# Expert bodies of a mixture-of-experts layer: down products and scatter moved one body later, two weight loads moved earlier

## The chip, the cores and the metric

The kernel runs on one core of a Trainium2 chip. The metric is the device time of one execution in microseconds. Before the change three runs gave 671.87, 671.91 and 672.01 us, median 671.91 us.

## The reference

One decoder layer over 512 tokens of width 1024, in float32. An attention branch and a gated linear attention branch are merged and added to the residual `h`; that part is not touched here. What follows is a mixture of experts: 4 groups of 8 experts, the best group, in it the two best experts.

```python
g_idx = argmax(xn @ router_group);  top_v, top_i = top_k(logits of that group, 2)
combine = softmax(top_v) * softmax(group logits)[g_idx]        # one weight per token and chosen expert
for g, e in 32 experts:                                        # FF = 256
    hg = silu(xn @ w_gate[g, e]) * (xn @ w_up[g, e])
    y += (hg * combine[:, g, e]) @ w_down[g, e]
return h + y
```

Each expert has 3 MiB of weights: gate, up and down, 1 MiB each. All 32 are read, 96 MiB.

## The kernel before

**Work.** Every expert takes up to 64 tokens (slots) in a round; the trace shows one round. Two experts stand side by side in one set of 128 slots and are called a pair; a body (`BODIES` = 8) works on two pairs, `s` = 0 and 1. In PE's order a body is:

1. gate and up products of pair 0, in two parts of 16 matmuls, into PSUM bank 0 (`expert_gate_up`, L990);
2. gate and up products of pair 1 into bank 1, and between their two parts the small products that give the row numbers and routing weights of the body after next (`slot_values`, L953), the transposes of the first pair's hidden rows (L998) and those of a one-hot matrix of slots (L960);
3. down products, 16 for each pair (L1004), with the second pair's hidden transposes among them;
4. transposes of the next body's gathered token rows (`row_transposes`, L984);
5. the scatter: 32 matmuls with the transposed one-hot matrix that put the slots' results back to their tokens (L1114), in two parts, `y_hi` and `y_lo`, whose sum is the float32 value.

Around PE: ScalarE takes SiLU of the gates (`hs`, L1452), copies the transposed hidden rows and one-hots out of PSUM (L1445, L1435), and rounds the down result to `y_hi` (L1465). VectorE multiplies `hs`, up product and routing weight (`hg`, L1880), forms `y_lo` (L1903), weights the transposed rows of the next body into `xgT` (L1862), adds the scattered rows to `h` (L1916), and builds one-hots (L1820) and row numbers (L1531, L1533). GpSimd gathers each pair's token rows from HBM by those row numbers (L2031). The eight PSUM banks are shared out by the constants `GU_BANK` to `LAST_BANKS`.

**Weights.** There is one buffer per pair of a body (`w_pair`), for gate and up together and for down. SyncE requests weights in a written order (`load`, L1146): when the gate products of pair `s` are done it loads the next body's gates of that pair (4 MiB), when the down products are done the next downs (2 MiB a pair). All go on one queue. The first body's weights lie in memory that the layer's earlier part still uses, so they are loaded in pieces as it comes free; down weights of its second pair come last, behind the picking of the first body's rows (`s_pick`, L943).

**Before the experts** the last token block is routed, the first body's rows are picked by matmuls with a one-hot matrix, and the routing weights of the last two blocks are formed on VectorE (`weigh`, the last line of it L1524), for which the products of the first slot weights (`first_slot_weights`) wait.

Of the kernel before, what the change touches and what calls it, by code (L numbers as in the profile page):

```python
# [53 lines left out]
H_BANK = (2, 3)  # L54
DOWN_BANKS = ((4, 5), (6, 7))
ROWS_BANKS = (0, 1, 2, 3)
W_BANKS = (4, 7)
OH_BANK = (5, 6)
SCATTER_BANKS = (4, 7, 5, 6)
LAST_BANKS = (0, 1, 2, 3, 4, 5, 6, 7)  # L60
# [197 lines left out]
def layer_kernel(nc, x, meta_tokens, norm1_w, w_in, q_norm_w, k_norm_w, attn_sinks, gla_gate_up, gla_gate_bias,  # L258
                 gla_norm_w, w_attn_branch, w_gla_branch, w_out, norm2_w, router_rows, norm2_rows,
                 expert_w_gate, expert_w_up, expert_w_down, table, triangle, rows_hbm, out):  # L260
    with ExitStack() as ctx:
# [138 lines left out]
        pause = more("pause", [P, 9])  # L400
# [6 lines left out]
        onehot = more("onehot", [P, NB, 2 * P], BF16)  # L407
# [190 lines left out]
        flipped = [tiles[k][:, 0:2 * P].bitcast(BF16) for k in OH_BANK]  # L598
# [5 lines left out]
        def _(pe):  # L604
# [343 lines left out]
            def oh(s, b):  # L948
                return onehot[:, b, s * P:(s + 1) * P]

            def slot_matmul(s, j, a, z):
                for b in range(NB):
                    last = nc.tensor.matmul(tiles[W_BANKS[s]][:, a:z], oh(s, b), info[:, b, 2 * j + s, a:z],  # L953
                                            start=(b == 0), stop=(b == NB - 1))
                return last

            def onehot_transposes(into=flipped):
                for s in range(2):
                    for b in range(NB):
                        last = nc.tensor.transpose(into[s][:, b * P:(b + 1) * P], oh(s, b), ident_b[:, :])  # L960
                    last.then_inc(s_ohTm[s], 1)
# [4 lines left out]
            onehot_transposes(first_flipped)  # L966
            pe.wait_ge(s_rounds, 1)
            rounds = pe.value_load(rounds_i[0:1, 0:1], min_val=1, max_val=T // SLOT)
            with pe.Fori(0, rounds) as r:
# [5 lines left out]
                def row_transposes(j):  # L975
                    for s in range(2):
                        pe.wait_ge(s_xg[s], 16 * (r * BODIES + j))
                        for half in range(2):
                            g = 2 * s + half
                            if j == BODIES:  # L980
                                pe.wait_ge(s_add[g], (r + 1) * (2 * BODIES))
# [14 lines left out]
                def hidden_transposes(s):  # L996
                    for f in range(2):
                        last = nc.tensor.transpose(tiles[H_BANK[s]][:, f * P:(f + 1) * P], hg[s][:, f * P:(f + 1) * P], ident)  # L998
                    last.then_inc(s_hTm[s], 1)
# [31 lines left out]
                def first_slot_weights():  # L1031
# [5 lines left out]
                    for s in range(2):  # L1037
                        pe.wait_ge(s_idx[s], r * BODIES + 1)
                        last = slot_matmul(s, 0, 2, 8)
                    last.then_inc(s_pwm, 1)  # L1040

                for i in range(BODIES):
                    n = r * BODIES + i

                    pe.wait_ge(s_xgT[0], n + 1)
                    pe.wait_ge(s_wgu[0], 64 * n + 64)
                    expert_gate_up(i, 0, 0)
                    if i == 0:
                        first_slot_weights()
                    pe.wait_ge(s_xgT[1], n + 1)  # L1050
                    expert_gate_up(i, 0, 1).then_inc(s_gu[0], 1)
                    if i == 0:
                        pe.wait_ge(s_pw, n + 1)
                        slot_values(1)
                        for s in range(2):
                            pe.wait_ge(s_ohT[s], n + 1)
                        onehot_transposes()
                    pe.wait_ge(s_xgT[2], n + 1)
                    pe.wait_ge(s_wgu[1], 64 * n + 64)
                    expert_gate_up(i, 1, 0)  # L1060
                    pe.wait_ge(s_xgT[3], n + 1)
                    for k in range(4):
                        pe.wait_ge(s_add[k], 2 * n + 1)
                    if i == 0:
                        pe.wait_ge(s_pw, n + 2)
                    if i + 2 < BODIES:
                        slot_values(i + 2)
                    elif i + 1 == BODIES:
                        for s in range(2):
                            pe.wait_ge(s_oh[s], n + 2)  # L1070
                            slot_matmul(s, 0, 0, 2).then_inc(s_tkm[s], 1)
                    pe.wait_ge(s_hg[0], n + 1)
                    hidden_transposes(0)
                    if i == 0:
                        for s in range(2):
                            pe.wait_ge(s_ohT[s], r * BODIES + 2)
                    if i + 2 != BODIES:
                        onehot_transposes()
                    expert_gate_up(i, 1, 1).then_inc(s_gu[1], 1)

                    if i + 2 < BODIES:
                        pe.wait_ge(s_pw, n + 3)
                        for s in range(2):
                            pe.wait_ge(s_ohT[s], r * BODIES + i + 3)
                    elif i + 1 == BODIES:
                        for s in range(2):
                            pe.wait_ge(s_idx[s], n + 2)
                            pe.wait_ge(s_ohT[s], n + 2)
                    pe.wait_ge(s_hT[0], n + 1)
                    pe.wait_ge(s_wd[0], 32 * n + 32)  # L1090
                    expert_down(0, 0)
                    pe.wait_ge(s_hg[1], n + 1)
                    hidden_transposes(1)
                    expert_down(0, 1).then_inc(s_down[0], 1)
                    pe.wait_ge(s_hT[1], n + 1)
                    pe.wait_ge(s_wd[1], 32 * n + 32)
                    expert_down(1, 0)
                    expert_down(1, 1).then_inc(s_down[1], 1)

                    if i + 1 == BODIES:  # L1100
                        last_scatter(i, n)
                        row_transposes(i + 1)
                        continue
                    row_transposes(i + 1)
                    for s in range(2):
                        pe.wait_ge(s_ylo[s], n + 1)
                    for u in range(8):
                        b, half = u // 2, u % 2
                        if u >= 4:
                            pe.wait_ge(s_add[u % 4], 2 * n + 2)  # L1110
                        cols_ = slice(half * 512, (half + 1) * 512)
                        for s in range(2):
                            for part in (y_hi, y_lo):
                                last = nc.tensor.matmul(tiles[SCATTER_BANKS[u % 4]][:, :], onehotT[i % 3][s][:, b, :],  # L1114
                                                        part[s][:, cols_], start=(s == 0 and part is y_hi),
                                                        stop=(s == 1 and part is y_lo))
                        last.then_inc(s_sc[u % 4], 1)

        @block.sync
        def _(sp):  # L1120
# [27 lines left out]
            def reload(i, n):  # L1148

                for s in range(2):  # L1150
                    sp.wait_ge(s_gu[s], n)
                    load(2 * i + s, s, True)
                for s in range(2):
                    sp.wait_ge(s_down[s], n)
                    load(2 * i + s, s, False)

# [10 lines left out]
            load(1, 1, True)  # L1167
            store_rows(NB - 1)
# [3 lines left out]
            load(1, 1, False)  # L1172
            with sp.Fori(1, BODIES) as i:
                reload(i, i)
            sp.wait_ge(s_rounds, 1)
            rounds = sp.value_load(rounds_i[0:1, 0:1], min_val=1, max_val=T // SLOT)
            with sp.If(rounds > 1):
                with sp.Fori(1, rounds) as r:
                    with sp.Fori(0, BODIES) as i:
                        reload(i, r * BODIES + i)  # L1180
# [9 lines left out]
        def _(act):  # L1190
# [29 lines left out]
            for step in SCHEDULE:  # L1220
# [186 lines left out]
                elif kind == "rowhi":  # L1407
                    b = step[1]
                    if b == NB - 1:
                        act.wait_ge(s_ohr, b)  # L1410
                        nc.scalar.activation(onehot[:, 0:b, :], onehot_r[:, 0:b, :].bitcast(F32), ACT.Copy).then_inc(s_cast, 1)
# [8 lines left out]
            nc.scalar.activation(onehot[:, NB - 1, :], onehot_r[:, NB - 1, :].bitcast(F32), ACT.Copy).then_inc(s_cast, 1)  # L1420
# [11 lines left out]
            def onehot_out(j, m, out_of=flipped):  # L1432
                for s in range(2):
                    act.wait_ge(s_ohTm[s], m + 1)
# [655 lines left out]
```

## Time and profile before

| | |
|---|---|
| median of the runs | 671.91 us |
| span of the profiled execution | 669.75 us (669.8 on the page) |
| PE busy | 650.2 us, 97% |
| PE in the chain that ended last | 87% of the span |
| VectorE, ScalarE busy | 390.7 us (58%), 215.9 us (32%) |
| expert weights requested | 96 loads of 1 MiB on SyncE's queue |
| rows gathered | 16 indirect DMAs, 3.64 MB |
| granted TensorE clock from 24 us on | 1.00 |

The span runs from the first to the last instruction of one profiled execution. Its share lines cut the span in 40 slices of 16.7 us; the experts fill about slices 25 to 40. "Busy" is the time in which an engine has an instruction at work; for PE the ends are modelled, so starts are the better measure of its pace.

### The profile page before, as it was taken

The numbers are of one execution on the slowest core, as the hardware profiler recorded it, in microseconds if no ns is written. First come the engines' busy times: TensorE is split into PE (matmuls) and PEld (weight loads), VectorE is DVE, ScalarE is ACT, GpSimd is POOL, SyncE is SP. The second block draws the span as 40 slices with busy tenths as digits, with TensorE's granted clock in tenths as the row PEclk, the third lists the DMA queues.
The fourth block names the chain that finished last, engine by engine and source line by source line (L and its number), as shares of the span: only waits on it lengthen the run. The fifth ranks groups of instructions, "written<-read, shape, count | busy, mean of one in ns | idle before, by whom it ended". The sixth has DMA issues, their size and how long they took to land.

```text
span 669.8 us, 10196 instructions
## 1 busy us (share of the span) xinstructions
PE 650.2 (97%) x3969; PEld 466.9 (70%) x3969; DVE 390.7 (58%) x736; ACT 215.9 (32%) x448; POOL 101.4 (15%) x138
## 2 busy tenths in 40 slices
PE   5799999999999999999989999999999999999998
PEld 3579999988888888888779995354544445453535
DVE  4648335678897878785674667453443535251615
ACT  6346232234534444422435565302020201110112
POOL 3300015899300000000000010110110101010010
PEclk9899999999999999999999999999999999999999
DMA  7432223202232121112345057999999999999943
GB/s 242 147 125 65 64 65 97 92 1 64 79 100 74 60 68 52 68 44 90 126 166 243 33 219 284 381 408 412 401 422 397 423 394 420 407 418 404 417 185 126
DMA packets 49794, 138.72 MB, mean 207 GB/s; under 512 B 6202, under 2 KB 28235, under 8 KB 41556
## 3 DMA queue, kind: packets, MB, share of 16 engines
q1 hardware_dynamic: 47298, 134.37, 52.8%
q0 software_dynamic: 2304, 3.64, 1.5%
q8 instruction: 32, 0.52, 0.3%
q14 instruction: 14, 0.11, 0.1%
q10 hardware_dynamic: 146, 0.07, 0.0%
HBM read 138.62 MB, written 4.19 MB: 213 GB/s over the span
## 4 chain that ended last, share of the span: by engine, by line
PE 87%; DVE 6%; ACT 3%; issue 2%; DMA 1%; POOL 0%; ACTq 0%; DVEq 0%
PE bank L990 16%; PE bank L608 12%; PE bank L609 12%; PE bank L610 12%; PE bank L1004 8%; PE bank L1114 8%; PE bank L850 1%; DVE y_lo L1903 1%; PE bank L1015 1%; PE bank L877 1%; PE bank L874 1%; ACT whi L1233 1%; DVE sig_a L1617 1%; DVE sig_a L1613 1%; DMA wraw<-in_w_out 1%
## 5 line engine op out<-in xcount | busy, mean ns | idle before, releaser
L990 PE MATMUL bank<-w_pair,xgT 128*64 128x512 f32 x512 | 113.8, 596 | 0.0
L990 PEld LDWEIGHTS bank<-w_pair,xgT 128*64 128x64 f32 x512 | 35.2, 137 | 66.4 <-issue 65.4
L1547 DVE TENSOR_TENSOR wlo<-wraw,whi 128x2048 fp32r<-128x2048 f32 (+1 forms) x25 | 56.4, 2258 | 20.3 <-ACT whi L1233 20.3
L608 PE MATMUL bank<-whi,xhi 128*128 128x256 f32 x224 | 64.4, 288 | 0.0
L609 PE MATMUL bank<-wlo,xhi 128*128 128x256 f32 x224 | 63.0, 281 | 0.0
L610 PE MATMUL bank<-whi,xlo 128*128 128x256 f32 x224 | 62.9, 281 | 0.0
L608 PE MATMUL bank<-xhi,whi 128*128 128x512 f32 x152 | 61.4, 404 | 0.0
L609 PE MATMUL bank<-xlo,whi 128*128 128x512 f32 x152 | 60.1, 396 | 0.0
L610 PE MATMUL bank<-xhi,wlo 128*128 128x512 f32 x152 | 59.7, 393 | 0.0
L1004 PE MATMUL bank<-w_pair,hT 128*64 128x512 f32 x256 | 58.1, 595 | 0.0
L1880 DVE SCALAR_TENSOR_TENSOR hg<-bank,pair_w,hs 128x256 f32<-128x256 f32 x16 | 7.7, 483 | 80.6 <-ACT hs L1452 80.6
L1233 ACT ACTIVATE whi<-wraw 128x2048 fp32r<-128x2048 f32 (+1 forms) x25 | 46.6, 1870 | 24.9 <-PE bank L617 11.1
L1452 ACT ACTIVATE hs<-bank 128x256 f32<-128x256 f32 x16 | 6.1, 384 | 135.5 <-PE bank L990 135.5
L1916 DVE TENSOR_TENSOR h<-h,bank 128x512 f32<-128x512 f32 x64 | 41.4, 681 | 7.5 <-PE bank L1114 6.0
L1114 PE MATMUL bank<-y_hi,onehotT 128*128 128x512 f32 x112 | 44.2, 394 | 1.5 <-DVE y_lo L1903 1.5
L1114 PE MATMUL bank<-y_lo,onehotT 128*128 128x512 f32 x112 | 43.7, 390 | 0.0
L1903 DVE TENSOR_TENSOR y_lo<-bank,y_hi 128x512 fp32r<-128x512 f32 x32 | 20.6, 685 | 39.2 <-ACT y_hi L1465 39.2
L608 PEld LDWEIGHTS bank<-whi,xhi 128*128 128x128 f32 x224 | 42.1, 188 | 1.8 <-issue 1.4
L610 PEld LDWEIGHTS bank<-whi,xlo 128*128 128x128 f32 x224 | 42.2, 188 | 0.0
L609 PEld LDWEIGHTS bank<-wlo,xhi 128*128 128x128 f32 x224 | 42.1, 188 | 0.0
L1004 PEld LDWEIGHTS bank<-w_pair,hT 128*64 128x64 f32 x256 | 17.7, 137 | 33.3 <-issue 33.3
L1927 POOL TENSOR_TENSOR pause<-pause 128x1 f32<-128x1 f32 x34 | 6.0, 196 | 223.0 <-PE bank L984 184.1
(331 smaller groups left out, 1330.9 us busy)
## 6 DMA issues: line engine op xcount, KB each, us to landing
w_pair<-in_expert_w_gate SPq DMA_DIRECT2D x32, 1024.0 KB
w_pair<-in_expert_w_up SPq DMA_DIRECT2D x32, 1024.0 KB
w_pair<-in_expert_w_down SPq DMA_DIRECT2D x32, 1024.0 KB, 17.4
wraw<-in_w_in SPq DMA_DIRECT2D x17, 1024.0 KB, 5.6
wraw<-in_w_out SPq DMA_DIRECT2D x4, 1024.0 KB, 5.3
h<-in_x SPq DMA_DIRECT2D x4, 512.0 KB, 5.3
wraw<-in_w_gla_branch SPq DMA_DIRECT2D x2, 1024.0 KB, 5.0
wraw<-in_w_attn_branch SPq DMA_DIRECT2D x2, 1024.0 KB, 5.2
```

The lines of the kernel that those rows point to most:

```text
L608: nc.tensor.matmul(ps, lhi(k), rhi(k), start=(k == 0), stop=False)
L609: nc.tensor.matmul(ps, lhi(k), rlo(k), start=False, stop=False)
L610: last = nc.tensor.matmul(ps, llo(k), rhi(k), start=False, stop=(k == kt - 1))
L850: nc.tensor.matmul(ps[:, 0:width], q, k, start=True, stop=True).then_inc(banks.done(("S", b, i, j)), 1)
L990: last = nc.tensor.matmul(tiles[GU_BANK[s]][j * SLOT:(j + 1) * SLOT, :].rearrange("p (f n) -> p f n", f=2), xgT[:, k, s * P + j * SLOT:s * ...
L1004: last = nc.tensor.matmul(tiles[DOWN_BANKS[s][half]][j * SLOT:(j + 1) * SLOT, :], hT[s][:, f, j * SLOT:(j + 1) * SLOT], we[s][j][2][:, f, ...
L1114: last = nc.tensor.matmul(tiles[SCATTER_BANKS[u % 4]][:, :], onehotT[i % 3][s][:, b, :], part[s][:, cols_], start=(s == 0 and part is y_hi ...
L1233: nc.scalar.activation(wh, raw, ACT.Copy).then_inc(s_hi, 1)
L1547: nc.vector.tensor_tensor(wl, raw, wh.bitcast(F32), ALU.subtract).then_inc(s_lo, 1)
L1880: nc.vector.scalar_tensor_tensor(hg[s][:, :], tiles[GU_BANK[s]][:, FF:2 * FF], pair_w[:, 2 * i + s:2 * i + s + 1], hs[s][:, :], ALU.mult, ...
L1903: last = nc.vector.tensor_tensor(y_lo[s][:, cols_], tiles[DOWN_BANKS[s][half]][:, :], y_hi[s][:, cols_].bitcast(F32), ALU.subtract)
L1916: nc.vector.tensor_tensor(h[:, b, cols_], h[:, b, cols_], tiles[bank][:, :], ALU.add).then_inc(s_add[u % 4], 1)
```

## The change

The order of PE, ScalarE, VectorE and SyncE in the experts is written anew. Down products and scatter of body `i` move into body `i + 1`; only body 0 keeps its own down products, and the last body does both its predecessor's and its own. Gate and up products of both pairs follow each other without anything between; hidden transposes of both pairs come together, into one bank shared with a down bank. Row numbers and one-hots of the body after next are formed at a body's end, from a second one-hot buffer. The slot weights of the first body come behind all gate products of its first pair. SyncE requests the first body's second pair's down weights before the last rows are stored, and the rest in the order in which the new bodies free their buffers.

```diff
-H_BANK = (2, 3)
+H_BANK = 5
-W_BANKS = (4, 7)
-OH_BANK = (5, 6)
+W_BANK = 2
+OH_BANK = 3
-        onehot = more("onehot", [P, NB, 2 * P], BF16)
+        onehot = [more(f"onehot{i}", [P, NB, 2 * P], BF16) for i in range(2)]
...
+                def down(i, n):
+                    for s in range(2):
+                        pe.wait_ge(s_hT[s], n + 1)
+                    for s in range(2):
+                        pe.wait_ge(s_add[s], 2 * n + 1)
+                        pe.wait_ge(s_add[s + 2], 2 * n + 1)
+                        pe.wait_ge(s_wd[s], 32 * n + 32)
+                        expert_down(s, 0)
+                        expert_down(s, 1).then_inc(s_down[s], 1)
...
+                for i in range(BODIES):
+                    n = r * BODIES + i
+                    if i + 1 == BODIES:
+                        down(i - 1, n - 1)
+                    pe.wait_ge(s_xgT[0], n + 1)
+                    pe.wait_ge(s_wgu[0], 64 * n + 64)
+                    expert_gate_up(i, 0, 0)
+                    pe.wait_ge(s_xgT[1], n + 1)
+                    expert_gate_up(i, 0, 1).then_inc(s_gu[0], 1)
+                    if i == 0:
+                        first_slot_weights()
+                        ...
+                        onehot_transposes(1)
+                    ...
+                    pe.wait_ge(s_wgu[1], 64 * n + 64)
+                    expert_gate_up(i, 1, 0)
+                    expert_gate_up(i, 1, 1).then_inc(s_gu[1], 1)
+                    if 2 <= i < BODIES - 1:
+                        down(i - 1, n - 1)
+                    if i >= 1:
+                        pe.wait_ge(s_ylo[0], n)
+                    if i + 1 < BODIES:
+                        hidden(n)
+                    if i == 0:
+                        ...
+                        slot_values(2)
+                        ...
+                        onehot_transposes(2)
+                        down(0, n)
+                    if i + 1 < BODIES:
+                        ...
+                        row_transposes(i + 1)
+                    if i >= 1:
+                        scatter(i - 1, n - 1)
+                    if i >= 1 and i + 2 < BODIES:
+                        ...
+                        slot_values(i + 2)
+                        ...
+                        onehot_transposes(i + 2)
+                    elif i + 1 == BODIES:
+                        ...
+                        onehot_transposes(0)
+                        down(i, n)
+                        ...
+                        last_scatter(i, n)
+                        row_transposes(i + 1)
...
+            def bodies_after_first(n):
+                next_gate_up(1, n + 1)
+                next_down(1, n + 1)
+                next_gate_up(2, n + 2)
+                with sp.Fori(2, BODIES - 2) as i:
+                    next_gate_up(i + 1, n + i + 1)
+                    next_down(i, n + i)
+                last = BODIES - 1
+                next_gate_up(last, n + last, (0,))
+                next_down(last - 1, n + last - 1)
+                next_gate_up(last, n + last, (1,))
+                next_down(last, n + last)
...
             load(1, 1, True)
+            load(1, 1, False, (0,))
+            sp.wait_ge(s_sq2, 4 * NB)
+            load(1, 1, False, (1,))
             store_rows(NB - 1)
             sp.wait_ge(s_pick[3], 1)
             sp.wait_ge(s_cast, 2)
             load(0, 0, False, (1,))
-            load(1, 1, False)
-            with sp.Fori(1, BODIES) as i:
-                reload(i, i)
+            bodies_after_first(0)
```

`next_gate_up(i, n)` waits for each pair until `n` bodies have done their gate products and requests the pair's gates of body `i`; `next_down` does so with down products and down weights. `scatter(i, n)` waits for both pairs' `y_lo` and issues the same 32 matmuls as before; in the last body the hidden transposes stand behind its second column block. ScalarE's and VectorE's orders follow PE's: `y_hi` and `y_lo` of body `i - 1` behind SiLU and `hg` of body `i`, then the rows of body `i + 1` into `xgT`, then the additions to `h`, then row numbers and one-hots.

## Rows read from the trace of the kernel before

**Rows 1.** The page, parts 1 and 2: busy share of PE; DMA in 40 slices

```profile
PE 650.2 (97%) x3969; PEld 466.9 (70%) x3969; DVE 390.7 (58%) x736; ACT 215.9 (32%) x448; POOL 101.4 (15%) x138
...
DMA  7432223202232121112345057999999999999943
GB/s 242 147 125 65 64 65 97 92 1 64 79 100 74 60 68 52 68 44 90 126 166 243 33 219 284 381 408 412 401 422 397 423 394 420 407 418 404 417 185 126
```

**Rows 2.** Waits of PE in the experts (405 to 670 us): total, times, longest

```profile
PE bank L1114 <- DVE y_lo L1903: 1.5, 7, 0.2
PE bank L953 <- DVE info L1524: 1.2, 1, 1.2
```

**Rows 3.** Stretches: length, busy by engine (instructions), granted clock, DMA share, GB/s

```profile
409.00:418.40 9.40, 8.16 (x58) 2.95 (x56) 6.22 (x27) 4.59 (x13) 0.19 (x1) 1.00 0.92 346
418.40:420.40 2.00, 2.00 (x22) 1.04 (x20) 1.46 (x8) 1.35 (x3) 0.19 (x1) 1.00 0.37 82
420.40:474.20 53.80, 53.37 (x284) 26.48 (x280) 25.93 (x56) 9.10 (x19) 8.05 (x16) 1.00 1.01 413
474.20:606.00 131.80, 130.94 (x674) 63.53 (x674) 56.47 (x117) 18.75 (x40) 10.76 (x24) 1.00 1.02 410
```

**Rows 4.** Timeline of PE: start, length, line; body 0's start, then body 1

```profile
409.42 3.65 PE L990 MATMUL bank<-w_pair,xgT 128*64 128x512 f32 x16
...
444.13 10.52 PE L990 MATMUL bank<-w_pair,xgT 128*64 128x512 f32 x48
454.59 0.36 PE L953 MATMUL bank<-info,onehot 128*128 128x8 bf16 x8
454.80 0.42 PE L998 MATMUL bank<-cst,hg 128*128 128x128 f32 x2
455.06 0.61 PE L960 MATMUL bank<-ident_b,onehot 128*128 128x128 bf16 x8
455.60 3.65 PE L990 MATMUL bank<-w_pair,xgT 128*64 128x512 f32 x16
459.08 1.89 PE L1004 MATMUL bank<-w_pair,hT 128*64 128x512 f32 x8
460.90 0.44 PE L998 MATMUL bank<-cst,hg 128*128 128x128 f32 x2
461.26 5.37 PE L1004 MATMUL bank<-w_pair,hT 128*64 128x512 f32 x24
466.57 1.97 PE L984 MATMUL bank<-cst,xg 128*128 128x128 f32 x16
468.75 0.47 PE L1114 MATMUL bank<-y_hi,onehotT 128*128 128x512 f32 x1 [0.21 <-DVE y_lo L1903]
...
476.19 10.52 PE L990 MATMUL bank<-w_pair,xgT 128*64 128x512 f32 x48
```

**Rows 5.** Timelines of ACT and DVE: SiLU, `hg`, `y_lo`, rows into `xgT`

```profile
459.30 0.38 ACT L1452 ACTIVATE hs<-bank 128x256 f32<-128x256 f32 x1 [2.68 <-PE bank L990]
459.71 0.48 DVE L1880 SCALAR_TENSOR_TENSOR hg<-bank,pair_w,hs 128x256 f32<-128x256 f32 x1 [3.32 <-ACT hs L1452]
467.31 1.29 DVE L1903 TENSOR_TENSOR y_lo<-bank,y_hi 128x512 fp32r<-128x512 f32 x2 [2.15 <-ACT y_hi L1465]
436.44 2.47 DVE L1862 TENSOR_TENSOR xgT<-bank,norm 128x512 f32<-128x512 f32 x4
```

**Rows 6.** Timeline of SyncE's DMA issues: body 1's first gates

```profile
418.46 0.37 SPq L1146 DMA_DIRECT2D w_pair<-in_expert_w_gate  x1
```

**Rows 7.** DMA queues from 418.4 to 474.2 us: packets, MB, share of 16 engines

```profile
q1 hardware_dynamic: 3428, 21.08, 92.6%
q0 software_dynamic: 644, 1.23, 5.8%
```

**Rows 8.** Timeline of PE and a stretch, early in the layer

```profile
20.44 3.56 PE L636 MATMUL bank<-xhi,gdp 128*48 128x512 f32 x8 [3.91 <-DVE xlo L1565]
23.80 2.08 PE L640 MATMUL bank<-xhi,whi 128*128 128x512 f32 x8
...
20.00:24.00 4.00, 3.56 (x9) 1.90 (x10) 3.35 (x5) 0.10 (x2) 1.32 (x3) 0.57 0.90 299
```

**Rows 9.** Timeline: the last scatter, the row transposes behind it, ScalarE's last work

```profile
658.26 0.50 PE L1015 MATMUL bank<-y_hi,onehotT 128*128 128x512 f32 x1
665.66 1.91 PE L984 MATMUL bank<-cst,xg 128*128 128x128 f32 x16
666.73 2.17 ACT L1470 ACTIVATE xgT<-bank,norm 128x128 f32<-128x128 f32 x8 [7.27 <-PE bank L984]
```

More of the change, by code:

```diff
@@ L399, in layer_kernel @@
         row_block = more("row_block", [P, 2])
-        pause = more("pause", [P, 9])
+        pause = more("pause", [P, 11])
         pair_w = more("pair_w", [P, PAIRS])
@@ L597, in layer_kernel, with slots, scatter_bank, hidden_bank @@
         first_flipped = [tiles[FIRST_FLIP_BANK][:, s * 2 * P:(s + 1) * 2 * P].bitcast(BF16) for s in range(2)]
-        flipped = [tiles[k][:, 0:2 * P].bitcast(BF16) for k in OH_BANK]
+        flipped = [tiles[OH_BANK][:, s * 2 * P:(s + 1) * 2 * P].bitcast(BF16) for s in range(2)]
+        def slots(j, s):
+            c = 32 * (j % 2) + 16 * s
+            return tiles[W_BANK][:, c:c + 8]
+        def scatter_bank(i, u):
+            if i + 1 == BODIES:
+                return tiles[LAST_BANKS[u]]
+            return tiles[LATE_BANKS[u % 4] if i + 2 == BODIES else SCATTER_BANKS[u % 4]]
+        def hidden_bank(s):
+            return tiles[H_BANK][:, s * 2 * P:(s + 1) * 2 * P]
         block = ctx.enter_context(nc.Block())
@@ new lines, in hidden @@
+                def hidden(n):
+                    for s in range(2):
+                        pe.wait_ge(s_hg[s], n + 1)
+                        hidden_transposes(s)
+                def down(i, n):
+                    for s in range(2):
+                        pe.wait_ge(s_hT[s], n + 1)
+                    for s in range(2):
+                        pe.wait_ge(s_add[s], 2 * n + 1)
[3 more added lines that the diff above has]
+                        expert_down(s, 1).then_inc(s_down[s], 1)
@@ L1105, in _, with scatter @@
+                def scatter(i, n):
                     for s in range(2):
@@ L1108, in _ @@
                         b, half = u // 2, u % 2
+                        if u == 2 and i + 2 == BODIES:
+                            hidden(n + 1)
+                        elif u == 2:
+                            for s in range(2):
+                                pe.wait_ge(s_hT[s], n + 2)
                         if u >= 4:
@@ L1466, in _ @@
                                                  tiles[DOWN_BANKS[s][half]][:, :], ACT.Copy).then_inc(s_yhi[s], 1)
+                for i in range(BODIES):
+                    n = r * BODIES + i
+                    if i + 1 == BODIES:
+                        high_rows(n - 1)
+                    for s in range(2):
+                        act.wait_ge(s_gu[s], n + 1)
+                        nc.scalar.activation(hs[s][:, :], tiles[GU_BANK[s]][:, 0:FF], ACT.Silu).then_inc(s_silu[s], 1)
+                        if s == 0 and i == 0:
+                            onehot_out(1, n + 1)
+                    if 2 <= i < BODIES - 1:
+                        high_rows(n - 1)
+                    for s in range(2):
+                        hidden_out(s, n)
+                    if i + 2 < BODIES:
+                        onehot_out(i + 2, r * BODIES + i + 2)
+                    elif i + 1 == BODIES:
+                        onehot_out(0, n + 1)
+                    if i == 0 or i + 1 == BODIES:
+                        high_rows(n)
                 for g in (1, 3):
@@ L1854, in slot_weights @@
                             last = nc.vector.tensor_reduce(pair_w[rows, 2 * j + s:2 * j + s + 1],
-                                                           tiles[W_BANKS[s]][rows, 2 + 3 * half:5 + 3 * half], AX.X, ALU.add)
+                                                           slots(j, s)[rows, 2 + 3 * half:5 + 3 * half], AX.X, ALU.add)
                     last.then_inc(s_pw, 1)
@@ L1898, in _ @@
                             build_onehot(0, s)
[L1899 to L1917 removed]
+                low_rows(r * BODIES + BODIES - 1)
+                add_rows(BODIES - 1, r * BODIES + BODIES - 1)
                 rows_weighted(BODIES, (0, 2))
```

222 lines of the change are left out of this document (91 added, 131 removed).

## The prediction

> **What bounds the kernel now.** I read the page's first two parts, the waits of PE, a table of stretches, and then the timeline of one expert body. PE is busy 97% of the span; in the last 40% of it the DMA digits are 9 as well [rows 1]. So the experts have two candidates for a bound. The waits settle what PE loses there: seven waits for `y_lo`, 1.5 us in all, and one of 1.2 us for the routing weights in the first body [rows 2]. That is 2.7 us of some 257; nothing else on PE can be removed by a new order except small changes of kind between instructions. The stretches show the other side: from 420.4 us to 606 us the 16 DMA engines are busy 1.01 to 1.02 of the time at 410 to 413 GB/s [rows 3]. PE and the transfers are tied: a body lasts 32.06 us on PE (gate products of two bodies start at 444.13 and 476.19 [rows 4]), and a body's 12 MiB of weights plus 0.5 MB of gathered rows, 13.1 MB, takes 31.9 us at 411 GB/s. The weights are not waited for today only because each is requested long before its use. An order that asks for the same weights earlier has to be checked against that stream, and this is where I expect the change to be decided.
>
> **PE, one steady body.** From the starts in rows 4: 64 gate/up products 10.46 + 3.48 = 13.94 us; slot values 0.21; the two hidden transposes 0.26 and 0.36; one-hot transposes 0.54; 32 down products 1.82 + 5.31 = 7.13; row transposes with the wait for `y_lo` behind them 2.18; scatter 7.44. In the new body the down products are one run (7.1) and the four hidden transposes another (0.52), and both these and the row transposes lie between the last down product and the scatter. The 16 row transposes alone take 1.85 (their 1.97 us [rows 4] less the overlap at the end). `y_lo` is complete 2.03 us after the last down product was issued, the row transposes begin at 466.57 and `y_lo` ends at 467.31 + 1.29 = 468.60 [rows 4, 5]; the new cover is 0.52 + 1.85 = 2.37 us, so the wait of 0.21 us goes and nothing takes its place. The new body is 13.94 + 7.1 + 0.52 + 1.85 + 7.44 + 0.21 + 0.54 = 31.6 us, 0.46 less. The second wait that the order adds, `hidden` for `y_lo[0]`, is met: the first half of the down products ends 3.5 us before. The H bank shared with a down bank is why it stands there.
>
> **PE, filling and emptying the pipeline.** Start from 409.42 [rows 4]. Body 0: gate products of the first pair to 416.44, now without the 1.2 us wait, since the slot weights come behind all 32 of them; slot values, slot weights and one-hot transposes 1.02, to 417.46; second pair to 424.43. Now the hidden transposes follow the gate products at once, with no down products between: SiLU starts 0.22 us after the last product and `hg` is ready at 459.71 + 0.48, 1.11 us after PE's last gate product [rows 4, 5]. So PE stalls about 0.9 us, goes on at 425.6, does slot values and one-hot transposes, waits 0.3 us for ScalarE's copy of the hidden rows (my estimate from two 0.38 us copies like the SiLU's [rows 5]), and runs `down(0)` from 426.8 to 433.9. Behind the row transposes there is now no scatter; body 1 needs `xgT`, which VectorE weights after `y_lo`, and the first of its four pieces is done 0.6 us after 436.44 [rows 5], or 2.6 us after the down products. Body 1 starts at 436.5: another 0.7 us stalled. The scatter that used to stand there was its cover; without it body 0 gains 0.15 us, not the 1.2 us. Body 1 has no down products: 13.94, the `hg` stall with the transposes 1.3, rows 1.85, scatter 7.44, slots 0.75: body 2 would start at 461.8, where the old one starts at 476.19. This is what the pipelining does to the weights.
>
> **The weights at body 2.** The first pair's buffer is free at 416.44, so SP issues at 416.7 instead of 418.46 [rows 6], 1.7 us earlier. The two down loads moved ahead (2 MiB) only make the queue empty by then; before, they ended with that issue, so this edit gives no more than the 1.7 us that the body gives. They pass one thing on SP, the store of the last routed rows at 407.2: the added wait for the squares is over at 400, and the store may land 1 to 2 us later, which the gather, at 419 at the earliest, covers. If that cover is gone, the same 1 to 2 us fall on the row transposes of body 0. From there the order is fixed by buffers: body 1's gates (8 MiB), body 1's downs (4 MiB), body 2's gates (8 MiB). Before, 418.4 to 474.2 us moved 21.08 MB of weights (20 MiB are 20.97 MB) and 1.23 MB of gathers [rows 7]; the last of the 20 MiB is out at about 474.1, 9 us before the second pair's products (476.19 + 6.97 = 483.2) want it. The new stream: 474.1, less 1.7 for the issue, less 0.4 because the queue never runs dry between bodies 1 and 2, plus 0.5 because the third body's gather (0.48 MB, a third of the three) falls wholly into it: 472.5, and with the landing 472.8. The 16 MiB up to the first pair's are in about 10 us earlier (4 MiB at 413 GB/s), near 462, just as PE arrives. PE arrives at the second pair at 461.8 + 6.97 = 468.8. It stalls 4.0 us.
>
> The trace gives 413 GB/s for this stream over 53.8 us [rows 3]. The Trainium skill (DMA: Bandwidth & Descriptors, Specifications) names an HBM limit of about 358 GB/s per core and a fabric ceiling of 435. By the lower one the stall would be some 12 us and the kernel near 682; the trace contradicts it, so it gets no weight. By the ceiling the stall would be 1.2 us and the kernel near 671; no row here shows that rate.
>
> **After the stall** PE is alone again. Second pair to 479.8, rest of body 2 (7.1 + 2.37 + 7.44 + 0.75) to 497.5; three bodies of 31.6 to 592.3; body 6, without slots, 30.85, to 623.15. Body 7: `down(6)` 7.1, gates 13.94, scatter with hidden transposes 7.96, slots and one-hots 0.75, `down(7)` 7.1, to 660.0; last scatter 7.4 and 4.09 from its end to the span's end, both as before (658.26 to 665.66 to 669.75 [rows 9]). Sum 671.5, 1.75 above the profiled span of 669.75. The stream is not late again: gates for body 4 can be asked for at 504.7 and take 10 us of the 24 us until use; downs of body 6 land about 5 us before body 7 opens.
>
> **TensorE's clock.** PE was idle for 3.91 us ahead of its product at 20.44, and the granted clock then averaged 0.57 from 20 to 24, with eight products of 512 columns taking 3.56 us against 2.08 for the next eight [rows 8]; the level had fallen to 1.2 GHz, which cost 1.5 us. A stall of 4.0 us is a little longer than that idle; the wait of 1.2 us in the first body left it at 1.00 [rows 2, 3]. The price lies between 0 and 1.5; since part of the fall may lie in the idle time, I take 0.8. The Trainium skill (TensorE: Matmul & The Clock Gate, What's actually happening) says that an idle array is put back to 1.2 GHz; by that alone the full price of that row would be due and the time 675.2.
>
> Sum: 669.75 + 1.75 + 0.8 = 672.3 span. The median of the runs lies 2.16 us above the profiled span (671.91 against 669.75), so **674.5 us**, 0.4% slower.
>
> **Rivals.** *Weights in time.* If body 2 finds its weights, the stall and the clock go: 671.5 - 4.0 + 2.16 = 669.7, faster by 0.3%, the most the PE order can give. For it: 9 us of lead today. Against: PE asks 14.4 us earlier while the stream starts 1.7 us earlier. It decides where the stall is under 1 us. *A short stall.* If the stream runs all through at the page's best slice, 423 GB/s, its 22.4 MB take 1.3 us less; if PE comes to body 2 a microsecond later than I add up, the stall is 1.5 to 2.7 us and the gains of the steady bodies cancel it: 671 to 672.5, no difference. For it: five of the page's slices in the experts stand at 417 to 423; against: 53.8 us on end at 413 [rows 1, 3]. *The stream stays late.* A body of 31.6 us on PE is shorter than the 31.9 us of its transfers; and near 504 the stream runs empty just as PE frees body 3's gate buffer, which costs the 1.9 us from issue to flow (418.46 to about 420.4 [rows 3, 6]). If this lag eats the 12 to 14 us of lead, every later body waits for the difference, 0.3 to 0.9 us in each of four, and the time is 676 to 678. Against: by these numbers the lag grows by 2 to 4 us only.
>
> **How the numbers follow.** My forecast 0.62, its own range 672.4 to 676.8 (stall 3 to 5.5, clock 0 to 1.5); weights in time 0.13; short stall 0.15; stream late 0.10. The range 669.6 to 678.0 leaves out half of the first rival and the top of the last. No change means within 0.2%, 670.57 to 673.25, about what this measurement can tell. Faster: 0.13 and a little of the second rival, 0.15. Same: the rest of it and the low end of my own case, 0.20. Slower 0.65.
>
> **What would show it.** In the changed profile: a PE idle of 3 to 5.5 us before the gate products of body 2's second pair, put down to a weights DMA; idle before hidden transposes in bodies 0 and 1 near 0.9 us; body 2 opening near 462; steady bodies of 31.6 us with no wait for `y_lo`; a dip of the granted clock near 473 or none. I am wrong if no gate product waits for weights, if steady bodies stay at 32.06, or if waits appear between row transposes and scatter.

## The result, and the profile after

The changed kernel takes 674.37 us (median of 10 runs, 673.6 to 675.16) against 672.25 us for the kernel before (median of 10 runs on the same chip, 671.35 to 672.89). The ratio is 1.0032, 95% interval 1.0024 to 1.0041: slower by 0.3%. Forecast was 674.5 us. As a change that is 2.6 us more than the 671.91 us known then; measured beside each other, the two kernels differ by 2.1.

One thing first about spans. The profiled execution of the changed kernel has a span of 672.9 us, 3.1 more than that of before, but body 0 starts at 410.34 us instead of 409.42 [rows 4]. Nearly all of these 0.92 us are not the change's. The granted clock is TensorE's clock as a share of 2.4 GHz; its other level is 1.2 GHz, 0.50, and a value between the two is a mean over a stretch. Over the first 30 us it is 0.89 in this execution and 0.94 in that of before, and among the profiles of this study the executions with 0.94 start body 0 at 409.3 to 410.0 us and those with 0.89 at 410.3 to 410.8, whichever kernel it is. So traces are compared here from body 0's first gate product to the end: 260.3 us before, 262.6 after, 2.2 more, which agrees with the runs. Runs scatter for this reason too: each run's mean granted clock is on record, and runs of one kernel differ by about 1 us with it (the changed kernel averages 673.78 us in its five runs at 0.995 and 674.80 in its three at 0.992), so some runs below are compared at like clock.

The first two views are the page of the changed kernel (parts 1 and 2) and PE's waits in its experts (total, times, longest), to be held against [rows 1, 2]. In these views PE is TensorE, PEld its weight loads, ACT is ScalarE, DVE VectorE, POOL GpSimd and SPq SyncE's queue of requests.

```profile
PE 648.3 (96%) x3969; PEld 471.1 (70%) x3969; DVE 392.1 (58%) x736; ACT 215.1 (32%) x448; POOL 104.2 (15%) x138
...
PEclk9799999999999999999999999999899999999999
DMA  7442223302232221112345067999898999999943
GB/s 241 146 125 64 63 64 95 94 1 63 82 101 69 63 64 62 64 52 74 126 185 221 33 249 289 418 411 417 350 415 347 415 417 410 421 407 414 416 169 126
```

```profile
PE bank L1005 <- DMA w_pair<-in_expert_w_up: 5.5, 2, 4.3
PE bank L1013 <- DVE hg L1965: 1.3, 2, 0.6
PE bank L1005 <- DVE xgT L1923: 0.8, 1, 0.8
PE bank L1019 <- ACT hT L1499: 0.5, 1, 0.5
```

The waits for `y_lo` and for the routing weights have gone, as they were meant to. In their place PE waits 8.1 us, of which 5.5 for weights from DMA (`w_up` is the last that the products wait for; gate and up together are called gate weights here); the page also shows the granted clock falling in the 29th slice (the 8 in PEclk, where all from the third slice on are 9 otherwise). PE's timeline of bodies 0 to 3 (start, length, line; the idle time before in brackets) says where; the scatters between are left out.

```profile
410.34 7.09 PE L1005 MATMUL bank<-w_pair,xgT 128*64 128x512 f32 x32
...
426.40 0.44 PE L1013 MATMUL bank<-cst,hg 128*128 128x128 f32 x2 [0.64 <-DVE hg L1965]
...
427.98 7.09 PE L1019 MATMUL bank<-w_pair,hT 128*64 128x512 f32 x32 [0.49 <-ACT hT L1499]
435.00 1.96 PE L999 MATMUL bank<-cst,xg 128*128 128x128 f32 x16
437.76 13.95 PE L1005 MATMUL bank<-w_pair,xgT 128*64 128x512 f32 x64 [0.80 <-DVE xgT L1923]
...
464.11 7.09 PE L1005 MATMUL bank<-w_pair,xgT 128*64 128x512 f32 x32 [1.26 <-DMA w_pair<-in_expert_w_up]
475.47 8.78 PE L1005 MATMUL bank<-w_pair,xgT 128*64 128x512 f32 x32 [4.27 <-DMA w_pair<-in_expert_w_up]
484.05 7.07 PE L1019 MATMUL bank<-w_pair,hT 128*64 128x512 f32 x32
...
501.35 13.95 PE L1005 MATMUL bank<-w_pair,xgT 128*64 128x512 f32 x64
515.14 7.04 PE L1019 MATMUL bank<-w_pair,hT 128*64 128x512 f32 x32
522.10 0.66 PE L1013 MATMUL bank<-cst,hg 128*128 128x128 f32 x4
522.60 1.91 PE L999 MATMUL bank<-cst,xg 128*128 128x128 f32 x16
524.29 0.47 PE L1092 MATMUL bank<-y_hi,onehotT 128*128 128x512 f32 x1
...
531.63 0.35 PE L968 MATMUL bank<-info,onehot 128*128 128x8 bf16 x8
531.85 0.61 PE L975 MATMUL bank<-ident_b,onehot 128*128 128x128 bf16 x8
532.38 1.08 PE L1005 MATMUL bank<-w_pair,xgT 128*64 128x512 f32 x4
```

PE is ready for body 2 at 464.11 - 1.26 = 462.85, waits, works 7.09 us, waits 4.27 us more, and then does 32 products in 8.58 us (475.47 to 484.05) that take half of 13.79 = 6.89 in a later body: 1.69 us lost to the clock. From body 3 on nothing is waited for, and a body lasts 31.03 us (501.35 to 532.38) against 32.06 before [rows 4]. The chain of waits passes the second stall through the transfer itself, asked for at 453.07 and landed 22.26 us later; the stretches (columns as in [rows 3]) show a full stream before it and the half clock behind it.

```profile
453.07 22.26 DMA w_pair<-in_expert_w_up
475.33 0.14 issue
475.47 8.78 PE bank L1005 x32
```

```profile
421.90:462.30 40.40, 37.84 (x212) 19.00 (x209) 16.31 (x34) 5.71 (x13) 3.75 (x8) 1.00 1.02 417
...
471.20:475.47 4.27, 0.00 (x1) 0.03 (x1) 0.48 (x1) 0.38 (x1) 0.00 (x0) 1.00 0.99 377
475.47:479.40 3.93, 3.93 (x12) 1.46 (x14) 0.00 (x0) 0.00 (x0) 0.00 (x0) 0.57 1.02 425
```

### The profile page after: what moved, and what is told of

It reads as the page before. It is cut to its first block, busy times and chain, and to the rows that moved or that the text cites. A ratio compares the mean times of both kernels' runs of the same rounds, so it can differ in the third digit from the quotient of the medians.

```text
span 672.9 us, 10163 instructions
## 1 busy us (share of the span) xinstructions
PE 648.3 (96%) x3969; PEld 471.1 (70%) x3969; DVE 392.1 (58%) x736; ACT 215.1 (32%) x448; POOL 104.2 (15%) x138
## 3 DMA queue, kind: packets, MB, share of 16 engines
q1 hardware_dynamic: 47298, 134.37, 52.4%
## 4 chain that ended last, share of the span: by engine, by line
PE 86%; DVE 5%; DMA 4%; ACT 3%; issue 2%; POOL 0%; SPq 0%; ACTq 0%; DVEq 0%
PE bank L1005 16%; PE bank L623 12%; PE bank L624 12%; PE bank L625 12%; PE bank L1019 8%; PE bank L1092 7%; DMA w_pair<-in_expert_w_up 3%; PE bank L865 1%; PE bank L999 1%; PE bank L1030 1%; PE bank L892 1%; PE bank L889 1%; ACT whi L1288 1%; DVE sig_a L1678 1%; DVE sig_a L1674 1%
## 5 line engine op out<-in xcount | busy, mean ns | idle before, releaser
L1005 PEld LDWEIGHTS bank<-w_pair,xgT 128*64 128x64 f32 x512 | 37.2, 138 | 76.6 <-issue 74.6
L1019 PE MATMUL bank<-w_pair,hT 128*64 128x512 f32 x256 | 56.5, 593 | 0.6 <-ACT hT L1499 0.5
L2002 POOL TENSOR_TENSOR pause<-pause 128x1 f32<-128x1 f32 x34 | 8.8, 270 | 226.8 <-PE bank L999 126.2
```

The costliest lines, as they stand in the source:

```text
L1005: last = nc.tensor.matmul(tiles[GU_BANK[s]][j * SLOT:(j + 1) * SLOT, :].rearrange("p (f n) -> p f n", f=2), xgT[:, k, s * P + j * SLOT:s * ...
L1019: last = nc.tensor.matmul(tiles[DOWN_BANKS[s][half]][j * SLOT:(j + 1) * SLOT, :], hT[s][:, f, j * SLOT:(j + 1) * SLOT], we[s][j][2][:, f, ...
L2002: return nc.gpsimd.tensor_tensor(o, a, b, op)
```

## The experiments

My theory: body 2's gate weights come late because the new order brings PE to them some 14 us earlier while the 4 MiB of body 1's down weights still stand ahead of them; the stall also costs clock; the steady bodies are faster. The rival: the whole difference is spread over the new waits in bodies 0 and 1 and the stream's rate, so that moving one request, or keeping PE busy, gives little. The experiments were timed beside the kernel before, whose median was 672.02 us in the session of e1 to e4 and 671.56 in that of e6 to e10; the first row is the result above. The ratios are the measure across sessions. The last two columns are read from each trace as above, from body 0's start to the end.

| kernel | runs, us | ratio to before, 95% | body 0 to end, us | against before |
|---|---|---|---|---|
| changed kernel | 674.37 | 1.0032 (1.0024 to 1.0041) | 262.6 | +2.2 |
| e1: split request | 669.70 | 0.9968 (0.9955 to 0.9981) | 258.1 | -2.2 |
| e2: filler | 672.29 | 1.0004 (0.9995 to 1.0012) | 261.2 | +0.9 |
| e3: no early loads | 675.53 | 1.0048 (1.0035 to 1.0061) | 263.0 | +2.7 |
| e4: early loads only | 672.45 | 1.0001 (0.9992 to 1.001) | 260.4 | +0.1 |
| e6: e1 without early loads | 669.99 | 0.9976 (0.9967 to 0.9985) | 258.3 | -2.0 |
| e7: e1 and a steady end | 668.37 | 0.9948 (0.9936 to 0.9961) | 256.5 | -3.8 |
| e9: e7, second `y_lo` wait later | 667.31 | 0.9939 (0.9926 to 0.9952) | 256.1 | -4.2 |
| e10: e9, rows ahead of `y_lo` | 667.96 | 0.994 (0.9928 to 0.9952) | 256.0 | -4.3 |

**e1, split request.** The changed kernel, but the down weights of body 1's second pair are asked for behind body 2's gate weights.

```
-            def next_down(i, n):
+            def next_down(i, n, sides=(0, 1)):
...
-                next_down(1, n + 1)
+                next_down(1, n + 1, (0,))
                 next_gate_up(2, n + 2)
+                next_down(1, n + 1, (1,))
```

> The changed kernel with one edit: SyncE requests the down weights of body 1's second pair (2 MiB) behind body 2's gate weights instead of ahead of them. Theory (late weights): body 2's second gate products waited 4.3 us, its first 1.3 us, and the clock fell for 1.7 us, all because 4 MiB of down weights stood ahead in the queue. With 2 MiB of them moved behind, the last gate weights land 5 us earlier, the wait at the second pair goes, the first pair's too, the clock stays, and 7.2 us come back: 667 us, faster than the kernel before by 0.7%. Rival (hand-offs): the cost is the short waits in bodies 0 and 1 (0.6, 0.6, 0.5 and 0.8 us, 2.6 in all) and the order of two loads matters little: 673 to 674 us.

Both stalls of body 2 are gone and the clock stays at 1.00 through it. But the time is 669.7, not 667: PE now waits for down weights where body 7 opens with `down(6)`. The waits, and the two places on PE's timeline:

```profile
PE bank L1019 <- DMA w_pair<-in_expert_w_down: 2.9, 2, 1.5
...
463.26 13.95 PE L1005 MATMUL bank<-w_pair,xgT 128*64 128x512 f32 x64
...
619.21 3.65 PE L1019 MATMUL bank<-w_pair,hT 128*64 128x512 f32 x16 [1.36 <-DMA w_pair<-in_expert_w_down]
624.39 3.65 PE L1019 MATMUL bank<-w_pair,hT 128*64 128x512 f32 x16 [1.53 <-DMA w_pair<-in_expert_w_down]
```

So 5.53 us of stall and 1.69 of clock come back, and 2.9 are paid at the end: 4.3 net, and the traces differ by 4.5. The place of two requests (2 MiB) in the order makes the difference between slower and faster; the rival falls. Without the stall the stream stays late, which was the mechanism of my third rival, at one place instead of four.

**e2, filler.** The changed kernel, with 36 transposes of the identity, whose result nobody reads, ahead of body 2's wait for its second gate weights.

```
+                    if i == 2:
+                        for k in range(36):
+                            nc.tensor.transpose(tiles[GU_BANK[1]][:, k % 4 * P:(k % 4 + 1) * P], ident, ident)
```

> The changed kernel with 36 extra transposes of the identity on TensorE ahead of the wait for body 2's second gate weights, into the bank that these products then overwrite; they do nothing for the result. Theory: the gate products behind the wait took 8.78 us instead of 7.09 since the idle time brought the granted clock down; with the engine kept at work through some 4 us the clock stays at 1.00, the products take 7.1 us, the kernel 1.7 us less: 672.7 us. Rival: these products were slow because the transfers or the restart behind a wait slow them; then the filler changes nothing, 674.4 us, or costs what it overshoots the wait by.

PE's timeline and the stretch behind the stall:

```profile
463.40 7.09 PE L1005 MATMUL bank<-w_pair,xgT 128*64 128x512 f32 x32 [0.93 <-DMA w_pair<-in_expert_w_up]
470.42 4.15 PE L1116 MATMUL bank<-cst 128*128 128x128 f32 x36
475.11 7.09 PE L1005 MATMUL bank<-w_pair,xgT 128*64 128x512 f32 x32 [0.54 <-DMA w_pair<-in_expert_w_up]
```

```profile
475.00:479.00 4.00, 3.90 (x18) 1.35 (x20) 0.00 (x0) 0.00 (x0) 0.00 (x0) 1.00 1.01 416
```

The weights come as late as before (475.11 against 475.47, with body 0 0.38 us earlier in this execution), but the products behind the wait run at 1.00 and take 7.09 instead of 8.78. At this place the clock's price is 1.69 us. From body 0 to the end 1.4 us of it remain, since PE, which is earlier now, waits for down weights where body 7 opens:

```profile
PE bank L1019 <- DMA w_pair<-in_expert_w_down: 0.2, 1, 0.2
```

The medians of the runs differ by 2.1 us, in part because they mix clocks. The dip itself lowers a run's mean clock by about a step of the record, so the pairs to compare are e2 at 0.997 with the changed kernel at 0.995 (672.35 and 673.78 on average) and 0.995 with 0.992 (673.08 and 674.80): 1.4 and 1.7 us. The rival, slow transfers or a slow restart, falls: here too the products start behind a wait (0.54 us) and beside a full stream (416 GB/s), and run at full pace.

**e3 and e4, the early loads.** e3 takes them out of the changed kernel; e4 puts them alone into the kernel before.

```
-            load(1, 1, False, (0,))
-            sp.wait_ge(s_sq2, 4 * NB)
-            load(1, 1, False, (1,))
...
+            load(1, 1, False)
```

> The changed kernel without the early loads: the down weights of the first body's second pair are requested behind the picks again, as in the kernel before. Theory: the queue is then busy until about 419.6 us, so body 1's gates start to flow 0.3 to 0.7 us later and everything that body 2 waits for comes that much later: 674.7 to 675.1 us. Rival (the early loads disturb the picks, whose products took 0.95 us for eight instead of 0.91): 0.2 us comes back and 674.2 us or less.

> The kernel before with the early loads alone. Theory: nothing waits for these weights and the next gates are asked for only when the first products are done, so no change within 0.2 us, 672.2 us. Rival: the empty queue lets the whole stream of weights run ahead and shortens the bodies, 670 us or less; or the loads slow the picks, 672.5 us.

e4 shows nothing, as expected. In e3 PE's wait for gate weights grows from 5.5 to 6.1 us, and the trace is 0.4 us longer; the medians of the runs say 1.2 with overlapping intervals. All five runs of e3 stand at a granted clock of 0.992, and average 0.5 us more than the changed kernel's three there (675.29 and 674.80). So these loads are worth about half a microsecond, as the theory had it, and only where PE waits for the stream.

```profile
PE bank L1005 <- DMA w_pair<-in_expert_w_up: 6.1, 2, 4.7
```

**e6, split request without early loads.** The edits of e1 and e3 together; the request that is split is that for body 1's down weights, as in e1, the early loads are body 0's.

> The kernel with the split request (first body's second-pair down weights asked for behind the third body's gates), but without the early loads of the first body's second-pair down weights: they are asked for where the kernel before asks for them. Theory: with the split request the transfers bind at the end, where the last body's opening down products wait 2.9 us for weights; a stream that begins later is later there by the same, 0.5 to 1.1 us as it was without the split, so 670.2 to 670.8 us and longer waits at that place, none at body 2. Rival: the early loads mattered only through the stall at body 2; with that stall gone there is no difference, 669.7 us.

Neither holds whole. The traces lie 0.2 us apart and the medians of the runs 0.3, between the two forecasts (0.5 to 1.1, and nothing). PE waits 0.7 us at body 2, where I expected nothing, and 2.2 at the end: together 2.9, as in e1, but paid at two places. That it is the same lag of the stream fits these numbers; no run shows it by itself.

```profile
469.83 7.09 PE L1005 MATMUL bank<-w_pair,xgT 128*64 128x512 f32 x32 [0.68 <-DMA w_pair<-in_expert_w_up]
```

**e7, a steady end.** e1, and body 7 keeps the order of the bodies before it: `down(6)` and the hidden transposes behind its gate products, its gate weights asked for ahead of body 6's down weights.

```
...
-                    if i + 1 == BODIES:
-                        down(i - 1, n - 1)
...
-                    if 2 <= i < BODIES - 1:
+                    if i >= 2:
                         down(i - 1, n - 1)
...
-                    if i + 1 < BODIES:
-                        hidden(n)
+                    hidden(n)
...
-                with sp.Fori(2, BODIES - 2) as i:
+                with sp.Fori(2, BODIES - 1) as i:
...
-                next_gate_up(last, n + last, (0,))
-                next_down(last - 1, n + last - 1)
-                next_gate_up(last, n + last, (1,))
-                next_down(last, n + last)
+                next_down(BODIES - 1, n + BODIES - 1)
```

> The split request, and the last body treated like the steady ones: down products of body 6 behind body 7's gate products instead of ahead of them, hidden transposes behind those, weights of body 7's gates asked for ahead of body 6's downs. Theory (transfers bind only because body 7's opening down products want their weights 14 us earlier than in a steady body): the 2.9 us of waits there go; the scatter of body 6 then has only the hidden transposes (0.49 us) for cover and waits 1.5 us for y_lo. Net about 1.4 us less, 668.3 us. Rival (PE's body of 31.0 us is shorter than the transfers of a body, so the lag just moves to the next place): a wait for the gate or down weights of 1.5 to 3 us shows up elsewhere in body 7, and the time stays at 669.5 to 670.

The theory holds: the trace is 1.6 us shorter than e1's (forecast 1.4), no wait for weights is left, and the scatter of body 6 waits 1.53 us for `y_lo`, because no row transposes stand ahead of it in the last body.

```profile
639.26 0.47 PE L1090 MATMUL bank<-y_hi,onehotT 128*128 128x512 f32 x1 [1.53 <-DVE y_lo L1928]
```

**e9, the second `y_lo` wait later.** e7, and the scatter waits for the second half of `y_lo` only behind its first two products.

```
-                    for s in range(2):
-                        pe.wait_ge(s_ylo[s], n + 1)
+                    pe.wait_ge(s_ylo[0], n + 1)
...
+                            if u == 0 and s == 1:
+                                pe.wait_ge(s_ylo[1], n + 1)
```

> As the one with the steady end, and the scatter's wait for the second half of y_lo put behind its first two products, which use only the first half. Theory: 0.45 us of the 1.5 us wait in body 7 is covered, about 0.45 us less than that kernel, 667.9 us; steady bodies unchanged at 31.04. Rival: nothing, since the last body's end is set by ScalarE or the transfers: same time.

The wait falls from 1.53 to 0.97 us, and the trace by 0.4. The median of the runs is 1.1 us less, with overlapping intervals; at like clock it is 0.6 less (667.21 against 667.84 at 0.997, 668.13 against 668.69 at 0.995, two or three runs each). By its median it is the fastest of the kernels: 667.31 us, 0.6% faster than before.

**e10, rows ahead of `y_lo` in the first body.** e9, with two steps of VectorE exchanged in body 0.

```
-                        low_rows(n)
...
                         rows_weighted(i + 1)
+                    if i == 0:
+                        low_rows(n)
```

> As the one before it, and in the first body VectorE weights the next body's rows (xgT) ahead of y_lo instead of behind it. The prediction says that the stall of body 1's first gate product comes from y_lo standing ahead of xgT on VectorE. Theory: the first xgT piece is ready 1.3 us sooner, the stall of 0.8 us goes, about 0.75 us less, 667.1 us; body 2 finds its weights with little to spare and may wait up to 0.5 us. Rival: the stall stays since the row transposes themselves come last, or the gain comes back as a wait for weights at body 2: same time.

On PE the stall of 0.80 us ahead of body 1 is gone, and with it the order of the two on VectorE is shown as its cause. The time doesn't fall: `down(5)` in body 6 now waits for weights, and body 2's gate products, 13.95 us in e9, take 14.19.

```profile
436.25 13.95 PE L1005 MATMUL bank<-w_pair,xgT 128*64 128x512 f32 x64
...
461.26 14.19 PE L1005 MATMUL bank<-w_pair,xgT 128*64 128x512 f32 x64
...
603.34 3.65 PE L1019 MATMUL bank<-w_pair,hT 128*64 128x512 f32 x16 [0.26 <-DMA w_pair<-in_expert_w_down]
```

The extra 0.24 us in body 2 have no row of their own, but the trace places them: PE pauses between the two pairs' products, and the last landing signal of the second pair's weights came at 468.22, 0.14 ahead of that pair's first product at 468.36. Counted from body 0's start, e10 is 0.78 us ahead of e9 where body 1 begins (26.64 against 27.42), 0.58 ahead where body 3 begins, and 0.12 from body 7 to the end. Most of what PE gains in body 0 the stream takes back in two places. The runs show no difference from e9 either: 668.14 against 668.13 on average at a granted clock of 0.995.

## Why the prediction was right

The mechanism was the forecast one. The place of the stall, what ended it and the sign were right, by reasoning. That the time came within 0.2 us of 674.5 is luck: three sizes were off (stall and clock too small by 1.5 and 0.9 us, the gains of PE's order by 2.9), and their errors cancelled. In order, each measured from body 0's start, as in the trace of after:

| step | predicted, us | measured, us |
|---|---|---|
| body 0 to body 1 | 27.1 | 27.42 |
| PE ready for body 2 | 52.4 | 52.51 |
| last gate weights of body 2 landed | 63.4 | 64.99 |
| stalls of body 2 | 0 + 4.0 | 1.26 + 4.27 |
| clock behind the stall | 0.8 | 1.69 |
| steady body | 31.6 | 31.03 |
| `down(6)` to the last scatter | 36.85 | 36.39 |
| last scatter to the end | 11.49 | 11.56 |

**Bodies 0 and 1** came out as added up: `hg` stalls of 0.64 and 0.63 (forecast 0.9 each), `hT` 0.49 (0.3), `xgT` 0.80 (0.7). e10 shows that the last is due to `y_lo` ahead of `xgT`, as the prediction had it.

**The stall** was 1.5 us too small. The step that failed is the landing: I added 0.3 us from the last byte of 20 MiB to the last packet of the request. The DMA queues of the changed kernel, from just ahead of the issue (417.4) to the moment at which PE was ready for body 2 (462.85), and then to the landing of the second pair's weights (475.33):

```profile
q1 hardware_dynamic: 2863, 17.18, 93.1%
```

```profile
q1 hardware_dynamic: 3478, 21.68, 92.3%
```

At 462.85 the weight queue had moved 17.18 MB, which is more than the 16 MiB (16.78 MB) that body 2's first pair needs, and yet PE waited 1.26 us; at 475.33 it had moved 21.68 MB, 0.71 more than the 20 MiB (20.97 MB) in question. By the same view over shorter times, 16.79 MB were through by 461.9 and 20.98 by 473.6, which is 63.3 us from body 0's start; the forecast for the last byte, 472.5 - 409.42 = 63.1, was right. But the weights had landed at 464.06 and 475.33, some 2 us after as many bytes were through, and not 0.3, for which no row was given. Some of the 16 engines were already in the next request's data while others still carried this one, and a request has landed when the last engine has. The landing signals in the trace show this: for body 2's first pair all but four had come by 462.55, the last four at 463.01, 463.42, 463.84 and 464.06. Where the queue ran empty, ahead of the issue, the busy share of the engines likewise fell by steps: 0.72 over 414.0 to 414.5, 0.30 at 415.0, 0.05 at 415.8, nothing from 416.0. The rate itself was as assumed: 417 GB/s over 40.4 us, against 413 before [rows 3]. The Trainium skill (DMA: Bandwidth & Descriptors, Specifications) gives about 358 GB/s as the HBM limit of a core; the 417 GB/s here contradict that again, for a kernel on one core, and they come near what the skill's HBM Reference (Specifications (TRN2)) gives for a core that streams alone, about 425.

**The clock** cost 1.69 us, not 0.8: it had stood at 1.00 throughout the idle time (the stretch from 471.20) and fell only as PE went on, to 0.57, mostly the lower level of 1.2 GHz, for the first 3.93 us of work. So the allowance for a fall hidden in the idle time was wrong; the full price of [rows 8] was due, and e2 shows it taken away by itself. The trace of the kernel before could have told: over the 3.91 us of idle ahead of its product at 20.44 the clock stood at 1.00 as well (columns as in [rows 3]).

```profile
16.53:20.44 3.91, 0.00 (x1) 0.04 (x1) 3.91 (x8) 3.57 (x6) 0.00 (x0) 1.00 0.37 97
```

The Trainium skill (TensorE: Matmul & The Clock Gate, What's actually happening) says that an idle array goes back to 1.2 GHz; the trace agrees that the lower level follows an idle time, and shows it only once PE works again. The sum that the prediction gave by that rule, 675.2, came out 0.8 us too high because the gains that it missed (2.9 us) were larger than what it missed of the stall (1.5). The stall of 1.26 us left the clock at 1.00 (464.11 to 471.20).

**The steady body** gained 1.03 us, not 0.46, and this is what brought the sum back: three bodies at 0.57 give 1.7, the rest of body 2, body 6 and body 7 another 1.2. By starts, gate products went from 13.94 to 13.79, down products from 7.13 to 6.96, hidden transposes from 0.62 to 0.50, row transposes with the wait behind them from 2.18 to 1.69, the scatter from 7.44 to 7.34. The terms of the sum that were too large are the gate products (13.94), the down products (7.1), the row transposes (1.85) and the scatter (7.44). The starts in the traces tell why. Within a run of one kind the pace did not change: two gate or down products every 0.429 us, a scatter product every 0.227, a transpose every 0.109, before and after. The time goes at a change of kind: before, the last gate products of the first run (at 454.06) took 0.10 us more than the others and the first behind the break 0.05 more. The prediction names such small changes of kind, and gives them no price. So the gate products gain 0.15 us by not being broken in two (10.46 + 3.48), the down products 0.17 in the same way, and the scatter 0.09 because slot values follow it instead of gate products (its last step 0.23 instead of 0.32). Of the row transposes the wait of 0.21 and 0.28 more went.

**The rivals.** That the weights would be in time fell for this kernel; e1 makes it true, and its time of 669.7 us is the one forecast for that rival, though it is made up otherwise (faster bodies, and 2.9 us of waits at the end). That the stream stays late in every later body fell too, since the stall gave the stream its lead back; e1, e6 and e10 show the mechanism once the stall is gone. The early loads were given no gain of their own; e4 agrees, and e3 finds half a microsecond where PE waits for the stream.

Left open: what sets the 2 us between bytes and landing (all weight requests here are of 1 MiB, behind others of their kind), and whether e9 or e10 is the faster.

## What to carry to other kernels

Software pipelining moves work later on the engine, and by that the next stage's loads earlier: add up the bytes that stand in the queue ahead of each load against the new time of its use, and sort the requests by use, before you count the waits that it removes. Reckon a load as landed when the slowest of the engines has finished it, here some 2 us after as many bytes were through, and add to a TensorE stall of several microseconds the half clock that follows it (1.69 us behind 4.27 us of idle here, nothing behind 1.26). When engine and stream are as close as here (31.0 against 31.9 us a body), every microsecond saved on the engine has to be found in the stream's lead as well.

## What the runs showed of the hardware

The granted clock can fall after an idle time instead of in it: 1.00 over the 4.27 us of idle, 0.57 over the 3.93 us of full work behind it (in e3 likewise, 1.00 over 4.66 us of idle and 0.57 over the next 3.94), and 1.00 throughout when the idle was filled with transposes. The early part of the layer varies between executions by the same kind of fall: over the first 30 us the mean granted clock was 0.94 in some and 0.89 in others, with the start of the experts 0.3 to 1.5 us later, which is as much as some of the edits here are worth, so a single span should not be compared with another without it.
